# Building the whole 64x64 inverse ahead in a chunked delta-rule recurrence: four bursts of small products per chunk instead of five

## What is computed

```python
def step(S, inp):
    r_t, w_t, k_t, v_t, kk_t, a_t = inp
    sa = einsum('bhvk,bhk->bhv', S, -kk_t)
    S = S * w_t + sa[..., None] * (kk_t * a_t) + v_t[..., None] * k_t
    y = einsum('bhvk,bhk->bhv', S, r_t)
    return S, y
```

## Time and profile before

| | us |
|---|---|
| time, median of 3 runs (772.95 to 773.49) | 772.99 |
| time of the profiled execution | 773.59 |
| its span | 771.9 |
| PE busy in the span | 740.1 (96%) |
| DVE busy | 428.4 (56%) |
| ACT busy | 229.5 (30%) |

### The profile page before, as it was taken

How to read it: one execution, slowest core, us unless ns; L and a number is a source line. 1 busy time by engine, 2 the same in 40 slices (tenths; PEclk the granted TensorE clock), 3 DMA queues, 4 the chain that set the end, 5 groups by cost and what they waited for, 6 DMA issues and landing times.

```text
span 771.9 us, 19753 instructions
## 1 busy us (share of the span) xinstructions
PE 740.1 (96%) x8328; PEld 527.0 (68%) x8328; DVE 428.4 (56%) x862; ACT 229.5 (30%) x543; POOL 45.3 (6%) x53
## 2 busy tenths in 40 slices
PE   7999999999999999999999999999999699999995
PEld 5887787787778777778878878778887533333331
DVE  5956667788787675756565564465223442212146
ACT  5122222254523333333323344310031501111145
POOL 0000000000000000010000000000000112221221
PEclk9999999999999999999999999999999689999998
DMA  9562432531221101121442102183934789999965
GB/s 324 205 207 85 155 126 72 209 114 56 73 91 56 56 30 58 58 59 44 148 119 59 57 30 84 44 332 122 409 125 167 250 349 397 392 402 390 377 211 220
DMA packets 38135, 130.43 MB, mean 169 GB/s; under 512 B 6267, under 2 KB 16763, under 8 KB 33184
## 3 DMA queue, kind: packets, MB, share of 16 engines
q1 hardware_dynamic: 32544, 115.07, 40.1%
q0 software_dynamic: 5504, 14.10, 6.2%
HBM read 111.13 MB, written 18.66 MB: 168 GB/s over the span
## 4 chain that ended last, share of the span: by engine, by line
PE 86%; DVE 5%; DMA 4%; issue 2%; ACT 1%; POOL 0%; SPq 0%; POOLq 0%; DVEq 0%; ACTq 0%
PE psum L1457 23%; PE psum L1812 11%; PE psum L1438 11%; PE psum L2784 9%; PE psum L2818 4%; PE psum L1415 4%; DVE arena L2184 3%; PE psum L1402 2%; PE psum L1390 2%; PE psum L1664 1%; PE psum L2764 1%; PE psum L1678 1%; PE psum L1580 1%; PE psum L1675 1%; DMA u_rows<-arena 1%
## 5 line engine op out<-in xcount | busy, mean ns | idle before, releaser
L2184 DVE TENSOR_TENSOR arena<-arena 128x268 f32<-128x268 f32 (+13 forms) x322 | 176.5, 548 | 47.6 <-ACT arena L1911 28.3
L1457 PE MATMUL psum<-arena 128*128 128x268 f32 x784 | 188.4, 392 | 0.0
L1457 PEld LDWEIGHTS psum<-arena 128*128 128x128 f32 x784 | 145.6, 190 | 33.0 <-issue 6.7
L1911 ACT ACTIVATE arena<-psum 128x268 f32<-128x268 f32 (+7 forms) x207 | 83.0, 410 | 258.9 <-PE psum L1457 138.6
L1911 ACT ACTIVATE arena<-arena 64x256 f32<-64x256 f32 (+11 forms) x173 | 69.0, 430 | 104.1 <-PE psum L1824 57.7
L1438 PE MATMUL psum<-arena 128*128 128x260 f32 x392 | 96.9, 392 | 0.8 <-DVE arena L2184 0.6
L2184 DVE TENSOR_TENSOR arena<-psum,arena 128x256 f32<-128x256 f32 (+7 forms) x151 | 60.4, 405 | 55.5 <-PE psum L1678 12.4
L1812 PE MATMUL psum<-arena 128*128 128x260 f32 x384 | 88.3, 385 | 1.5 <-DVE arena L2184 0.8
L2784 PE MATMUL psum<-arena 128*32 128x512 f32 (+1 forms) x640 | 86.7, 604 | 0.5 <-DVE arena L2949 0.3
L1438 PEld LDWEIGHTS psum<-arena 128*128 128x128 f32 x392 | 70.9, 189 | 17.3 <-issue 5.4
L1812 PEld LDWEIGHTS psum<-arena 128*128 128x128 f32 x384 | 71.3, 190 | 15.4 <-DVE arena L2187 2.1
(11 more groups left out here) (233 smaller groups left out, 669.0 us busy)
## 6 DMA issues: line engine op xcount, KB each, us to landing
arena<-in_w_gu SPq DMA_DIRECT2D x16, 2048.0 KB, 19.7
arena<-in_w_in SPq DMA_DIRECT2D x45, 512.0 KB, 4.2
arena<-in_w_dn SPq DMA_DIRECT2D x16, 1024.0 KB, 17.2
arena<-in_w_out SPq DMA_DIRECT2D x2, 2048.0 KB, 14.9
arena<-in_x SPq DMA_DIRECT2D x8, 268.0 KB, 6.0
arena<-arena SPq DMA_DIRECT2D x16, 134.0 KB, 4.4
arena<-in_x SPq DMA_DIRECT2D x1, 2144.0 KB, 14.5
arena<-arena SPq DMA_DIRECT2D x4, 520.0 KB, 6.5
```

Of the source, the lines that this page charges most:

```text
L1457: last = mm(ps, w[:, k, :], x[:, k, :], start=(k == 0 and i in (0, 1, 3)), stop=(k == KD // 2 - 1), skip_group_check=i not in (0, 1, 3))
L1911: run(nc.scalar.activation(out, in_, fn, **kw), s)
L2184: run(v.tensor_tensor(out, a, b, op), s)
```

## The change

The 64x64 inverse of a chunk is completed before its chain needs it. A fifth `wk_x` (level 32) multiplies the off-diagonal block `below` with the first block's inverse, a new step `wk_u` multiplies that with the second block's, and ACT copies the pieces into a new buffer `inv` (`wk_w` four copies, `wk_u` two). `wk_sa` then is one step of eight 64x64 products, and `wk_y` and `wk_sb` are gone. Level 16 of `wk_t` now makes also the first block's plain inverse (eight products more). Three chunks are under way instead of two; `xl` and its PSUM columns are doubled. A chunk has four bursts, with 4, 4, 3 and 4 parts of other work between them. In front of chunk 0 stand nine bursts, of three rounds, the first after four parts and not six. DVE's reads of a burst wait for the burst's last `wk_x` or `wk_t` (and for `wk_d`).

```diff
-TAKES = (3, 3, 3, 3, 3)
-TAKES_AHEAD, TAKES_LAST = 2, (3, 3, 2, 2, 2)
+TAKES = (4, 4, 3, 4)
+TAKES_FIRST, TAKES_AHEAD, TAKES_LAST = 4, 2, (3, 3, 2, 3)
...
-        return [of(c, ("wk_t", 16)) + of(c + 1, ("wk_x", 4)) + of(c, ("wk_r",)) + of(c + 1, ("wk_k",)),
-                of(c + 1, ("wk_t", 4)) + of(c, ("wk_sa",)),
-                of(c, ("wk_y",)) + of(c + 2, ("wk_d",)) + of(c + 1, ("wk_x", 8)),
-                of(c + 1, ("wk_t", 8)) + of(c + 2, ("wk_x", 2)) + of(c, ("wk_sb",)) + of(c + 1, ("wk_a",)),
-                of(c + 2, ("wk_t", 2)) + of(c + 1, ("wk_x", 16)) + of(c, ("wk_s",))]
+        return [of(c, ("wk_r",)) + of(c + 2, ("wk_x", 2)) + of(c + 1, ("wk_x", 8)) + of(c, ("wk_x", H)) + of(c + 1, ("wk_a",)),
+                of(c, ("wk_u",)) + of(c + 1, ("wk_t", 8)) + of(c + 2, ("wk_t", 2)),
+                of(c, ("wk_sa",)) + of(c + 1, ("wk_x", 16)) + of(c + 2, ("wk_x", 4)) + of(c + 3, ("wk_d",)),
+                of(c, ("wk_s",)) + of(c + 1, ("wk_t", 16)) + of(c + 2, ("wk_t", 4)) + of(c + 2, ("wk_k",))]
...
-    s += take(6)
-    for c in range(-2, len(CHUNKS) - 1):
+    s += take(TAKES_FIRST)
+    for c in range(-3, len(CHUNKS) - 1):
...
+        between = [of(c + 3, ("wk_e",)) + (prep(c + 2, ("wk_p", 5)) if c + 2 else []) + of(c + 1, ("wk_b",), ("wk_m",), ("wk_l",))
+                   + prep(c + 3, ("wk_p", 0)),
+                   prep(c + 3, ("wk_p", 1), ("wk_p", 2), ("wk_p", 3), ("wk_p", 4)),
+                   so[0:1], of(c + 1, ("wk_v",), ("wk_w",)) + so[1:3]]
...
                 elif kind == "wk_t":
-                    if 2 * b < n:
-                        for p, s, d, g, rd in tiles_of(c):
-                            mm(psum[g, 2560 + H * p:2560 + H * p + n], tp[c % 3][g, 1, p, 0:n], xl[g, p, 0:n],
+                    for p, s, d, g, rd in tiles_of(c):
+                        if 2 * b < n or CHUNKS[c][1] == C and d == 0:
+                            mm(psum[g, o + H * p:o + H * p + n], tp[c % 3][g, 1, p, 0:n], xl[c % 2][g, p, 0:n],
...
+                elif kind == "wk_u":
+                    c = step[1]
+                    pe.wait_ge(s_xl, X_N[(c, H)])
+                    for p, s, d, g, rd in tiles_of(c):
+                        if d == 1:
+                            last = mm(psum[64 * s:64 * s + H, 3840 + H * p:3840 + H * p + H], tp[c % 3][g, 0, p, :],
+                                      tp[c % 3][g, 1, p, :], start=True, stop=True)
...
                 elif kind == "wk_sa":
+                    if CHUNKS[c][1] == C:
+                        pe.wait_ge(s_y1, 6 * (c + 1))
+                        for p in range(NP):
+                            for s in range(2):
+                                _, _, full, _ = wk(c, s)
+                                last = mm(psum[full, 3328 + 64 * p:3328 + 64 * p + 64], inv[full, p, :], rr[full, p, :],
+                                          start=True, stop=True)
```

More of the change, by code:

```diff
@@ L388, in order @@
         so = [("so", c + 1 - SMP_FROM, i) for i in range(3)] if 0 <= c + 1 - SMP_FROM < NP else []
[L389 to L395, removed]
+        between = [of(c + 3, ("wk_e",)) + (prep(c + 2, ("wk_p", 5)) if c + 2 else []) + of(c + 1, ("wk_b",), ("wk_m",), ("wk_l",))
+                   + prep(c + 3, ("wk_p", 0)),
+                   prep(c + 3, ("wk_p", 1), ("wk_p", 2), ("wk_p", 3), ("wk_p", 4)),
+                   so[0:1], of(c + 1, ("wk_v",), ("wk_w",)) + so[1:3]]
+        for i, x in {-2: ((2, 0), (3, 1)), -1: ((1, 2), (2, 3))}.get(c, ()):
+            between[i].append(("tg", x))
         for i, now_ in enumerate(bursts(c)):
-            if c == -2 and i < 2:
+            if c == -3 and i != 2:
                 continue
             s += now_
-            if i == 4 and c == 5:
+            if i == 3 and c == 5:
                 while not whole_job():
@@ L832, in hybrid_step, with burst_of, first_and_last @@
         X_N, T_N = count_of("wk_x"), count_of("wk_t")
+        def burst_of(step):
+            n0 = n1 = STEPS.index(step)
+            while STEPS[n0 - 1][0].startswith("wk_"):
+                n0 -= 1
+            while STEPS[n1 + 1][0].startswith("wk_"):
+                n1 += 1
+            return STEPS[n0:n1 + 1]
+        def first_and_last(step, count):
+            x = [count[s[1:]] for s in burst_of(step) if s[0] == step[0]]
+            return x[0] - 1, x[-1]
+        X_RUN = {x: first_and_last(("wk_x", *x), X_N) for x in X_N}
+        T_RUN = {x: first_and_last(("wk_t", *x), T_N) for x in T_N}
         PAB = {s: n + 1 for n, s in enumerate([s for s in STEPS if s[0] in ("wk_d", "wk_a")])}
@@ L2033, in _ @@
                     else:
[L2034 removed]
+                        act.wait_ge(s_ab, 2 * c - 1)
                     if c >= 4:
@@ L2064, in _ @@
                         act.wait_ge(s_act, own[0])
-                elif kind == "wk_b" and CHUNKS[step[1]][1] > H:
+                elif kind == "wk_b":
                     c = step[1]
@@ L2089, in _ @@
                     c = step[1]
-                    act.wait_ge(s_psa, 3 * c + 1)
+                    act.wait_ge(s_psa, 2 * c + 1)
                     f(rr, bank(6, 256).rearrange("t (p k) -> t p k", p=NP), s=s_rr)
-                elif kind in ("wk_sa", "wk_sb"):
+                elif kind == "wk_w":
                     c = step[1]
-                    act.wait_ge(s_psa, 3 * c + (2 if kind == "wk_sa" else 3))
-                    for s in range(2):
-                        x = slice(64 * s + (0 if kind == "wk_sa" else H), 64 * s + (min(CHUNKS[c][1], H) if kind == "wk_sa" else C))
+                    act.wait_ge(s_tt, T_N[(c, 16)])
+                    if c:
+                        act.wait_ge(s_psa, 2 * c)
+                    for p, s, d, g, rd in tiles_of(c):
+                        if p == 0:
+                            f(inv[g, :, rd], tp[c % 3][g, 1], s=s_y1)
+                elif kind == "wk_u":
+                    c = step[1]
+                    act.wait_ge(s_py, c + 1)
+                    for s in range(2):
+                        f(inv[half(s, H), :, H:C], psum[half(s, H), 3840:3968].rearrange("t (p k) -> t p k", p=NP), s=s_y1)
+                elif kind == "wk_sa":
+                    c = step[1]
+                    act.wait_ge(s_psa, 2 * c + 2)
+                    for s in range(2):
+                        x = half(s, CHUNKS[c][1])
                         nc.scalar.activation(vals[c % 2][x, :, s, :], psum[x, 3328:3584].rearrange("t (p k) -> t p k", p=NP),
@@ L2353, in _ @@
                 elif kind == "st0":
+                    for i in range(2):
+                        run(v.memset(inv[64 * i + H:64 * i + C, :, 0:H], 0.0))
                     job_done(dve, ("j_w", len(PAIRS) - 1, SEVEN - 1))
```

118 lines of the change are left out of this document (54 added, 64 removed).

## The result

| | before | after |
|---|---|---|
| median | 772.97 us (772.35 to 773.49, 4 runs) | 794.5 us (791.23 to 797.91, 4 runs) |
| ratio | | 1.0277, 95% interval 1.0251 to 1.0304 |
| span of the profiled execution | 771.9 us | 794.2 us |
| the recurrence in it, first part to last `wk_s` | 247.9 us | 264.4 us |

A forecast was written before the change was run, and what follows sets the result against it. PE's instruction time plus about 2.0 us of waits was taken as the bound; PE's work -3.5 and waits +2.8 made -0.7 us, so the median was forecast at 772.3 us, range 769.0 to 776.2.

The forecast's parts named there:

- The step that failed: Whole recurrence: its length is PE's instruction time plus about 2.0 us of waits, from three waits for DVE.
- its own sign of being wrong: Profile after: the forecast is wrong if PE stops somewhere not listed, such as at ACT's copies.
- Products: PE, all eight chunks: products removed 1.69 and added 1.38 us per chunk, together -2.5 us (-3.7 to -1.5).
- entries: PE going back to large products after a burst: 0.20 us each, seven bursts fewer, -1.4 us (0 to -1.6).
- +0.4 for shapes: PE changing tile shape after small products: at most one more place per chunk, +0.4 us (0 to +0.8).
- Waits in front of chunk 0: PE waiting for DVE at `wk_x`, `j_bon` and `wk_d` before chunk 0: 3.5 us, where before 1.1 + 0.3 stand.
- Within the chunks: PE waits after chunk 4's third burst, for `fs` 3, 0.8 us, and after chunk 1's, at `j_st`, 0.5 us.
- The rivals: DVE earlier, 769.5 us (chance 0.28); `wk_d` waits in chunks, 775.9 (0.13); entry cost stays, 775.1 (0.12); narrow products dear, 777.3 (0.03).

The follow-up runs named there:

- shifts of 64 and 128: Changed kernel with the first sixteen products of `wk_d` 0 issued twice (64 more PE instructions) or three times (128 more): 785.45 and 798.09 us.
- the padded kernel: Kernel before, with every `wk_x` 16 issued twice, so its largest burst has 354 instructions instead of 290: 783.88 us.
- the six bursts: Changed kernel with six bursts per chunk instead of four; `wk_r` with `wk_a`, and `wk_s` with `wk_k`, moved two parts later: 780.84 us.

## Why the prediction was wrong, point by point

**The step that failed** is in the first paragraph: "the stage lasts as long as PE's instructions take, plus about 2.0 us of waits". The list of waits of before also had two stops named "issue", 1.1 and 0.5 us; I listed the waits for DVE and left these out. They were the sign that PE's supply of instructions was just in time: in before, five block ends, two of them the stops, are passed 1.34 to 1.5 us after the packet's last byte, without slack. What the runs showed in its place: at block ends PE stands still for its instructions, 11.8 us in after, where the prediction had nothing, and this is 10.2 of the 16.5 us. The prediction named its own sign of being wrong, that PE stops somewhere that it had not listed, and that is what happened. The prediction then priced each burst by its passes (-0.2 us per burst that goes) and never counted instructions per burst. By the built programs the bursts before have 290, 179, 161, 226 and 258 instructions with three parts between them, and after 228, 290, 291 and 339; a middle chunk has 1,243 to 1,245 and 1,275 to 1,278. The second figure adds harm: 1,277 is nearly five blocks of 256, so a block ends at almost the same step in every chunk, in `wk_a` four times. That the size of the loss hangs on where the ends lie is shown by 785.45 and 798.09 us for shifts of 64 and 128. That longer bursts are its ground is supported by the padded kernel and the six bursts, but not shown: each of these edits also moved steps or block ends. Nor is a burst with two block ends the whole of it. In after only three stops, 2.7 of the 11.8 us, are at the second end within a burst; the four in `wk_a`, 5.7 us, are at the only end in a burst of 228.

**Products** (-2.5) and **entries** (-1.4, +0.4 for shapes): right in size, as the kernel with 64 more instructions shows them. `wk_sa` took 0.61, level 32 of `wk_x` 0.37 with the change of shape to `wk_a` in it (forecast 0.25 and up to 0.1), `wk_u` 0.16 (305.86 to 306.02) instead of 0.25. A middle chunk without a stop is 0.58 us shorter, forecast 0.45; a burst costs 0.25, forecast 0.20. PE's busy time with 64 more instructions is 244.8 us; less two dips (3.4), the added products (0.3) and the restart behind three stops (0.2 each) it is 240.5, 2.8 below before, forecast 3.5.

**What a stop costs beside itself** was no term at all: the restart of the pipeline, 0.2 us (the group of `wk_a` has 9.7 us busy before and 11.0 after, with four stops in it), and the dip of the clock. In fourteen traces the recurrence has 24 dips, 22 of 3.4 us and two of 6.8; each begins in a stop or wait (the shortest was 1.3 us) or at most 1.6 us behind it, but six others of that length in after alone had none.

**Waits in front of chunk 0**: right. Forecast 0.9, 0.25, 0.7 and 1.6 (the last by a slip: its own terms, 5.8 and 4.1, give 1.7); the list has 0.9 (`wk_x`), 0.3 and 1.7 (`wk_d`) and 0.7 (`j_bon`). **Within the chunks**: 0.8 and 0.5 forecast, 0.9 (L1455) and 0.6 (L1778) found. **Missed**: 2.0 us at L1432, a part of `j_bb` that waits for ACT at 472.38, in the one chunk where ACT has the first norms (`j_var`, `ln_r`) beside its copies. ACT loads a table there, 1.28 us from 470.55, directly ahead of the operation that PE waits for. Before does the same at 447.24, but there a burst that needs nothing of it comes next on PE. I had looked at ACT's mean (8 of 20 us busy) and not at that chunk. In the six-burst kernel, where `wk_w` stands two parts earlier and `wk_v` two later, it is 1.1; no run tried this wait alone. Waits together 7.1 against the 4.8 forecast.

**The rivals.** Each moved a term by a few us and none held the mechanism; the pricing of shapes and waits was sound and beside the point. Without stops the sum stands as it was put: PE -2.8 and waits +4.9 are about +2 us. No version here beats the kernel before. By this sum the change is worth nothing even with all stops gone, unless the waits of its deeper pipeline go too; no run had both gone.

**What stays open** is when a packet is asked for. In the four stops at `wk_a` it started 4.7 to 5.7 us behind the block end before, and 0.6 to 1.2 us after PE had passed the 64th instruction behind that end, as if the wide parts in between gave no time. In the three bursts of after with a stop at their second end it came 0.2, 1.4 and 0.4 us behind the first, and at other ends of the same recurrence up to 1 us ahead of the end before. What sets this no run shows: none changed that distance alone.

## What to carry to other kernels

Where a kernel issues many small matmuls, count PE's instructions per burst as well as their time, and see where each 256th (128 passes) falls. In the nine stops of after the block end before lay 2.8 to 8.2 us back, so neither that distance nor two ends in one burst tells by itself where PE will stop; the stops, 0.3 to 2.4 us long, all came at a block's end in or right behind a burst of small products. Look for "issue" among PE's waits before you make bursts denser. Wide work put ahead of a block's end helped here (5.7 to 0.6 us in `wk_a`). Give no verdict on such a change from one alignment: 64 instructions more at the start made this kernel 9 us faster. A stop also costs the restart and, in some cases, 1.7 us of slow clock behind it.

## What the runs showed of the hardware

- PE's instructions arrive during the run, in packets of 16,384 bytes on a DMA queue of their own, one per 256 instructions (68 in 794 us), each 0.88 to 2.1 us long. PE was never seen to pass a block's end sooner than 0.98 us after its packet's last byte, in over 800 cases.
- The Trainium skill (Trainium Architecture — The Big Picture, The software stack) has the instruction streams copied to the engines when a program is loaded; here PE's came all along the run, 41 packets of the 68 between 255 and 500 us, and their lateness cost over 10 us.
- Sixteen passes of 32 columns on two tiles took 0.16 us (`wk_u`), 10 ns a pass.
- In 24 cases PE's granted clock fell to the 1.2 GHz level in or up to 1.6 us behind a stop or wait of 1.3 to 3.3 us, 22 times for 3.4 us and twice for 6.8; the one whose passes were timed lost 1.7 us.
